# Four modulation blocks as matrix-vector products on TensorE, late squares on VectorE, and other slots for the later modulation blocks

## What is computed

```python
def ada_modulation(c, w, b, n_chunks):
    m = jax.nn.silu(c) @ w + b
    return jnp.split(m[:, None, :], n_chunks, axis=-1)
...
            shift, scale, gate = ada_modulation(c, a_ada_w[l], a_ada_b[l], 3)
            u = rms_norm(h, a_norm_g[l]) * (1 + scale) + shift
            q, k, v, z = jnp.split(u @ a_w_in[l], 4, axis=-1)
            q = rms_norm(q.reshape(bsz, seq, 2 * A_HEADS, A_HEAD_DIM), a_q_norm_g[l])
            k = rms_norm(k.reshape(bsz, seq, 2 * A_HEADS, A_HEAD_DIM), a_k_norm_g[l])
...
            o = diff_causal_attention(q, k, v, lam, slopes_a)
            o = rms_norm(o, a_subln_g[l]) * (1.0 - lambda_init)
            o = o.reshape(bsz, seq, A_INNER) * jax.nn.silu(z)
            h = h + gate * (o @ a_w_out[l])
            if layer == N_A_LAYERS - 1:
                kv_shift, kv_scale = ada_modulation(c, kv_ada_w, kv_ada_b, 2)
```

## Time and profile before

| | |
|---|---|
| runs | 1184.56 us median of 3 (1182.88 to 1186.97) |
| the profiled execution | 1183.36 us |
| its span | 1181.6 us |
| TensorE matmul | busy 1114.6 us (94%), 6120 |
| VectorE | busy 760.5 us (64%), 2483 |
| ScalarE | busy 666.3 us (56%), 2041 |
| GpSimd | busy 151.3 us (13%), 293 |
| chain that ended last | TensorE 85%, VectorE 6%, ScalarE 3%, issue 3%, DMA 2% |

### The profile page before, as it was taken

One profiled execution on the slowest core, in us unless ns is written; L12 is line 12 of the kernel. 1 busy time (PEld: TensorE's weight loads), 2 busy tenths in 40 slices (PEclk: granted clock), 3 DMA queues, 4 the chain that ended last, 5 costly groups with the idle time before them and its releaser, 6 DMA issues.

```text
span 1181.6 us, 19499 instructions
## 1 busy us (share of the span) xinstructions
PE 1114.6 (94%) x6120; PEld 887.1 (75%) x6120; DVE 760.5 (64%) x2483; ACT 666.3 (56%) x2041; POOL 151.3 (13%) x293
## 2 busy tenths in 40 slices
PE   1578999999999999999998999989999999999998
PEld 1466777777777777777777788878878778787887
DVE  6786787878878777877877444665555555556222
ACT  4565565666666566665665544666666666666010
POOL 1110111111111111011110111211111111110211
PEclk9988999999999999999999999999999999999999
DMA  9621222322223232222313634301111111113542
GB/s 360 226 81 50 87 73 87 97 64 81 80 90 95 72 100 66 88 81 88 98 54 95 199 102 131 125 19 35 45 43 41 41 41 41 41 50 112 161 143 89
DMA packets 65606, 108.47 MB, mean 92 GB/s; under 512 B 5600, under 2 KB 34400, under 8 KB 65248
## 3 DMA queue, kind: packets, MB, share of 16 engines
q1 hardware_dynamic: 65504, 107.23, 28.8%
HBM read 90.43 MB, written 16.78 MB: 91 GB/s over the span
## 4 chain that ended last, share of the span: by engine, by line
PE 85%; DVE 6%; ACT 3%; issue 3%; DMA 2%; SPq 1%; POOL 0%; DVEq 0%; ACTq 0%; POOLq 0%
PE ps_p L562 15%; PE ps_p L564 14%; PE ps_p L563 14%; PE ps_s L621 6%; PE ps_o L673 6%; PE ps_p L606 5%; PE ps_p L608 5%; PE ps_p L607 5%; PE ps_o L754 4%; PE ps_t L693 3%; PE ps_o L800 2%; PE ps_t L783 2%; PE ps_s L733 2%; DMA ada_in<-ada_w 1%; PE ps_o L647 1%
## 5 line engine op out<-in xcount | busy, mean ns | idle before, releaser
L562 PE MATMUL ps_p<-w_hi,u_hi 128*128 128x512 f32 x768 | 337.7, 440 | 21.9 <-DVE u_lo L1228 21.9
L564 PE MATMUL ps_p<-w_hi,u_lo 128*128 128x512 f32 x768 | 304.5, 396 | 0.0
L563 PE MATMUL ps_p<-w_lo,u_hi 128*128 128x512 f32 x768 | 303.9, 396 | 0.0
L562 PEld LDWEIGHTS ps_p<-w_hi,u_hi 128*128 128x128 f32 x768 | 146.5, 191 | 66.9 <-issue 23.2
L564 PEld LDWEIGHTS ps_p<-w_hi,u_lo 128*128 128x128 f32 x768 | 146.0, 190 | 32.9
L563 PEld LDWEIGHTS ps_p<-w_lo,u_hi 128*128 128x128 f32 x768 | 147.3, 192 | 17.4
L958 ACT ACTIVATE e<-e,negm 128x256 f32<-128x256 f32 (+7 forms) x128 | 98.4, 769 | 82.8 <-DVE negm L1293 81.6
L1182 DVE TENSOR_TENSOR w_lo<-raw,w_hi 128x512 fp32r<-128x512 f32 x120 | 82.8, 698 | 43.0 <-ACT w_hi L869 43.0
L495 POOL TENSOR_SCALAR gbuf<-gbuf 128x128 f32<-128x128 f32 (+1 forms) x96 | 32.9, 343 | 541.9 <-ACT gbuf L896 541.9
L995 ACT ACTIVATE pT<-ps_t 128x512 f32<-128x512 f32 (+2 forms) x96 | 44.5, 490 | 75.1 <-PE ps_t L693 74.6
L673 PE MATMUL ps_o<-va,pT 128*128 128x128 f32 x576 | 78.4, 281 | 0.0
(11 more groups left out here) (184 smaller groups left out, 2148.9 us busy)
## 6 DMA issues: line engine op xcount, KB each, us to landing
adabuf<-ada_w SPq DMA_DIRECT2D x48, 512.0 KB, 3.9
raw<-w_a SPq DMA_DIRECT2D x76, 256.0 KB, 3.9
raw<-w_b SPq DMA_DIRECT2D x44, 256.0 KB, 3.1
ada_in<-ada_w SPq DMA_DIRECT2D x7, 1024.0 KB, 13.4
x_in<-x SPq DMA_DIRECT2D x8, 512.0 KB, 12.5
oa_scratch<-gbuf SPq DMA_DIRECT2D x64, 64.0 KB, 1.6
late<-oa_scratch SPq DMA_DIRECT2D x8, 512.0 KB, 4.5
stage<-x SPq DMA_DIRECT2D x8, 512.0 KB, 4.9
```

The lines of the kernel that those rows point to most:

```text
L562: pe.matmul(o, u_hi[:, c, t], w_hi[par][:, c, :], start=(c == 0), stop=False)
L563: pe.matmul(o, u_hi[:, c, t], w_lo[par][:, c, :], start=False, stop=False)
L564: mm = pe.matmul(o, u_lo[:, c, t], w_hi[par][:, c, :], start=False, stop=(c == KD - 1))
```

## The change

Four of the first 16 blocks (1, 4, 7, 10) are computed on TensorE: their weights are stored transposed, TensorE multiplies each of a block's eight 128 x 128 parts with one column of silu(c), and VectorE adds the bias to the four columns at once. Weight chunks 0 to 3 and x tiles 2 and 3 are loaded behind the last block. The roots of x tiles 0 and 1 are made after block 5 instead of 3, those of tiles 2 and 3 behind the splits of the first head's weights instead of after block 8, with their squares and normalising on ScalarE. ScalarE and VectorE split all weight chunks behind smod; VectorE modulates x tile 1 before the low parts. The squares of x tiles 4 to 7 go to VectorE, two ahead of the attention and two in slot 1. The 48 later blocks are not worked on in the first head; the other heads have seven each, in slots 0 to 6, and the last has six.

```diff
-ADA_UNIT = 6
+ADA_UNIT = 7
+ADA_LATER = 48
+
+ADA_PE = (1, 4, 7, 10)
...
+def later_block(u, i):
+
+    k = ADA_UNIT * (u - 1) + i
+    return k if u > 0 and i < ADA_UNIT and k < ADA_LATER else None
...
-                    if is_a and live(0) and i < ADA_UNIT:
-                        k = ADA_UNIT * u + i
+                    if is_a and live(0) and later_block(u, i) is not None:
+                        k = later_block(u, i)
...
             for j in range(0, ADA0 - 2, 2):
                 sp.dma_start(ada0_in[:, j:j + 2, :], ada_w[j:j + 2].rearrange("a p n -> p a n")).then_inc(ada0_loaded[j // 2], 16)
-                if j < 8:
+                if j < 4:
                     load_x(j // 2)
-                if j in (8, 10):
-                    for c in (j - 8, j - 7):
-                        load_chunk(0, c, w_a[0, :, c, :])
             for j in (ADA0 - 2, ADA0 - 1):
                 sp.dma_start(ada0_in[:, j, :], ada_w[j]).then_inc(ada0_loaded[j + 1 - ADA0 // 2], 16)
+            for c in range(RAW):
+                load_chunk(0, c, w_a[0, :, c, :])
+            for n in (2, 3):
+                load_x(n)
             for c in range(RAW, KD):
                 load_chunk(0, c, w_a[0, :, c, :])
...
+            for j in ADA_PE:
+                pe.wait_ge(ada0_loaded[j // 2], 16)
+                for d in range(KD):
+                    mm = pe.matmul(ps_p[:, 0, j:j + 1], ada0_in[:, j, d * P:(d + 1) * P], csil[:, d:d + 1],
+                                   start=(d == 0), stop=(d == KD - 1))
+                mm.then_inc(s_ctr, 1)
             for n in range(2):
...
                     if isinstance(u, int) and u == 0 and 1 <= i < NT - 1:
                         x_modulate(i + 1)
+                        if i == 1:
+                            x_seed(2)
...
-            for k in range(2):
+            def x_rows_done(k):
                 for n in range(*x_groups[k]):
                     x_squares(n)
                 x_seed(k)
                 for n in range(*x_groups[k]):
                     x_normalise(k, n)
-            for c in range(RAW):
-                split_hi(0, c, 0)
+
+            x_rows_done(0)
             act.wait_ge(s_mod, 1)
             x_modulate(0)
-            for c in range(RAW, KD):
+            for c in range(2):
                 split_hi(0, c, 0)
             x_modulate(1)
-            for n in range(*x_groups[2]):
-                x_squares(n)
-            x_seed(2)
+            for c in range(2, KD):
+                split_hi(0, c, 0)
+            x_rows_done(1)
             attn_a(a, A_HEADS, 0)
...
+            def x_squares(n):
+
+                dve.wait_ge(n_x[n], 16)
+                dve.wait_ge(n_ss, n)
+                dve.tensor_tensor_reduce(e1[:, :].rearrange("p (a n) -> p a n", n=FW), x_rows(n), x_rows(n), 1.0, 0.0,
+                                         ALU.mult, ALU.add, xss[:, n:n + 1]).then_inc(n_ss, 1)
...
                     if first and 1 <= i < NT - 1:
                         x_modulate(i + 1)
+                    if first and i == 1:
+                        x_squares(6)
+                        x_squares(7)
+                        x_roots(2)
...
-                    if live(0) and i < ADA_UNIT:
-                        k = ADA_UNIT * u + i
+                    if live(0) and later_block(u, i) is not None:
+                        k = later_block(u, i)
...
             for j in range(ADA0):
-                dve.wait_ge(ada0_loaded[max(j // 2, j + 1 - ADA0 // 2)], 16)
-                modulation(ada0_in[:, j, :], j, ada0_done)
-                if j in (3, 8):
-                    x_roots((j - 3) // 5)
+                if j not in ADA_PE:
+                    dve.wait_ge(ada0_loaded[max(j // 2, j + 1 - ADA0 // 2)], 16)
+                    modulation(ada0_in[:, j, :], j, ada0_done)
+                if j == 5:
+                    x_roots(0)
...
-                if j >= ADA0 - RAW:
-                    split_lo(0, j - ADA0 + RAW, 0)
-            dve.wait_ge(ada0_done, ADA0)
+
+            dve.wait_ge(s_ctr, 1 + len(ADA_PE))
+            t = slice(ADA_PE[0], ADA_PE[-1] + 1, 3)
+            dve.tensor_tensor(mod[:, t], ps_p[:, 0, t], prm[:, C_ADAB + t.start:C_ADAB + t.stop:3], ALU.add).then_inc(ada0_done, 1)
+            dve.wait_ge(ada0_done, ADA0 - len(ADA_PE) + 1)
...
             x_modulate(0)
+            x_modulate(1)
             x_low(0)
-            for c in range(RAW, KD):
+            for c in range(KD):
                 split_lo(0, c, 0)
-            x_modulate(1)
             x_low(1)
-            x_roots(2)
+            x_roots(1)
+            dve.wait_ge(bias_step, 2)
+            x_squares(4)
+            x_squares(5)
             attn_a(a, A_HEADS, 0, M_A_GATE, 0)
```

More of the change, by code:

```diff
@@ L1621, in _ @@
             x_modulate(0)
+            x_modulate(1)
             x_low(0)
-            for c in range(RAW, KD):
+            for c in range(KD):
                 split_lo(0, c, 0)
-            x_modulate(1)
             x_low(1)
-            x_roots(2)
+            x_roots(1)
+            dve.wait_ge(bias_step, 2)
+            x_squares(4)
+            x_squares(5)
             attn_a(a, A_HEADS, 0, M_A_GATE, 0)
-            dve.wait_ge(ada_done, ADA_UNIT * A_HEADS)
+            dve.wait_ge(ada_done, ADA_LATER)
             dve.scalar_tensor_tensor(out=smod[:, 1, :], in0=mod[:, M_KV_SCALE:M_KV_SCALE + KD], scalar=1.0,
@@ L1661 @@
     ada_w = np.concatenate([f["a_ada_w"][0], f["kv_ada_w"], f["b_ada_w"][0]], axis=1)
-    ada_w = ada_w.T.reshape(-1, P, D)
+    ada_pe = ada_w.reshape(KD, P, -1, P).transpose(2, 1, 0, 3).reshape(-1, P, D)
+    ada_w = ada_w.T.reshape(-1, P, D).copy()
+    ada_w[list(ADA_PE)] = ada_pe[list(ADA_PE)]
     wa_in = f["a_w_in"][0].reshape(D, 4, A_HEADS, P).transpose(0, 2, 1, 3).reshape(D, 4 * D)
```

## The result

The changed kernel takes 1176.72 us, median of 8 runs (1174.74 to 1180.13); beside it on the same chip the kernel before took 1184.33, median of 8 (1178.61 to 1186.97). The ratio is 0.9948 [0.993, 0.9966]: **faster by 7.6 us**, clear of the noise though only 0.5%, where 2.9 were forecast. The median lies 1.9 us under the low end of the range. The profiled execution took 1174.74 us, the fastest of the eight. The changed kernel's times stand in groups (four at 1174.7 to 1175.3, two at 1178.1, then 1179.3 and 1180.1), so the median depends on how many runs fell into which. In a later session of 12 runs the median was 1179.44 against 1183.62 (experiment 9); over all 23 executions of this kernel it is 1178.40, against 1183.65 over 77 of the kernel before (one more of those, a slow one at 1269.59, is left out). The typical gain is thus about **5.2 us**.

A forecast was written before the change was run, and what follows sets the result against it. It took TensorE as the bound in seven heads, and waits in the opening and first head. 2.2 us to tile 1's end plus 0.7 from the clock made 2.9 off the median 1184.56: 1181.7 us, range 1178.6 to 1185.0.

The forecast's parts named there:

- the 7.8 us: Opening: modulation starts near 30.8 instead of 38.63; the queue behind smod leaves 1.6 us of it at x rows 2.
- an upper bound of 1.97: Opening: a modulation block on TensorE takes at most the 1.97 us of eight transposes; 1.9 us was taken, at no cost.
- the term 2.2: Up to the end of tile 1: query and key transposes at 58.3, 2.2 us earlier (1.7 to 2.8).
- I take the restart as slow until 50: Behind the hole in TensorE's queue: matmuls from 45.0 run at half clock until 50, between 48.7 and 51.1.
- the clock term 0.7: Slot 3: one idle stretch instead of two, so slow matmuls for nearer 3.8 than 5.8 us; 0.7 us gained.
- 1 us either way: Later slots of the first head: allowance on the total for where the clock falls there.
- Rival (1): Slot 3: the clock holds across the one idle stretch; gain 2.2 + 2.9 and 0.6, 1178.9 us; chance 0.15.
- Their going is worth nothing: Slots 3 to 5 of the first head: removing the later blocks gains nothing, as other chains set those slots.
- 0.6 us of idle time left: Heads 2 to 7: VectorE's 1.85 us idle covers the seventh block's 1.2 us, so it costs nothing.
- rival (4): Later heads: the seventh block delays the sums, qn and TensorE; 7.2 us lost, 2.9 gained, 1188.9 us; chance 0.05.
- (2): Restart behind the hole: TensorE runs at full pace from 45.0, tile 0 ends 2.4 us better; 1179.3 us; chance 0.08.
- (3): Opening: weights 4 to 7 come late, the hole is longer and eats the 2.9 us; 1184.5 us; chance 0.12.

The follow-up runs named there:

- experiment 9: The changed kernel again, unedited, in a later session: median 1179.44 us over 12 runs; its trace is of the fastest run.
- kernel 16: The kernel before, unedited, traced once more: 1183.30 us.
- kernel 6: The changed kernel with products of zeros in TensorE's idle stretches of the first head and 14 in the hole of slot 1: 1173.95 us.
- kernel 13: The changed kernel, unedited, another trace, from the middle group of times: 1177.83 us.
- kernel 1: The changed kernel with the later modulation blocks six a head again, from the first head on: 1181.20 us.
- 4: The kernel before with TensorE's idle stretches filled by 16, 16, 16 and 10 products that add zeros, which outlasted the stretches: 1182.88 us.
- kernel 2: The kernel before with only the later blocks moved, none in the first head and seven in the others: 1180.94 us.
- kernel 3: The kernel before with only the squares of x tiles 4 to 7 moved to VectorE, the roots behind them: 1185.16 us.
- 5: The kernel before with fewer products of zeros in TensorE's idle stretches (7, 8, 8 and 6): 1178.93 us.
- 12: The changed kernel with tile 0 projected whole before x rows 2 are transposed and the square of x tile 4 on ScalarE, without fillers: 1175.62 us.
- 14: The changed kernel, unedited, a further trace: 1179.33 us.
- 15: The changed kernel, unedited, a further trace: 1178.40 us.

## Why the prediction was wrong

The direction was right, and so was the working of the opening. Two terms of the sum were too small, and a loss was in no term. The median of the later session, 1179.44, lies inside the stated range; that would have been luck, for these errors partly cancel.

**Opening.** The last block was forecast to end at 30.3 and smod to be used at 30.8; it ended at 29.98 and the use came at 30.30. First matmul: 35.4, measured 34.95. Nine matmuls, then a hole until 45.0: a wait of 5.59 us until 44.43. qn: 54.4, measured 54.48 as its end. That most of the 7.8 us would go in the queue behind smod held: 8.3 us at smod, 2.2 at x rows 2. A block on TensorE took 3.5 us (6.99 for two, 3.57), where eight transposes gave an upper bound of 1.97. The bound was wrong: each of the eight products is recorded twice, so a block is 16 matmuls and 16 loads, not eight, and 16 loads at the pace of the row of eight make 3.9. It cost nothing, since block 10 ended at 26.1 and x rows 0 and 1 were transposed by 29.6, still before 30.30.

**To the end of tile 1**, the term 2.2. Measured: query and key transposes at 56.91 instead of 58.3, 3.6 us before the old 60.51. Of the 1.4 missed, 0.6 is the earlier restart; most of the rest is "I take the restart as slow until 50". The matmuls became fast at 48.27, 3.8 us after the restart, not 5.0. In the kernel before, 6.1 us had passed, in its slot 5, 3.8, and in kernel 16, the same program as before, 3.1 after the start at 42.38. So no one figure would have served; only the bounds could, and 3.8 lies near their early end. The hole was a loss that the change made for itself: the last of the nine matmuls ahead of it were fast, the first five behind it slow, and filling the hole (kernel 6) gave back 1.4 us at slot 3. The Trainium skill ("TensorE: Matmul & The Clock Gate", What's actually happening) says that half clock is the default and activity releases it; the trace agrees, with a clock of 0.50 at 42 and of 1.00 again from 50.

**From slot 3 on**, the clock term 0.7, is the step that failed. It said that the clock falls again at slot 3, for a shorter time, and dismissed the later slots with "1 us either way". In the profiled execution there was no fall at all from slot 3 to slot 8, worth 7.2 us. In typical ones there were two instead of four, worth 4.0, and there the step splits: at slot 3 it came true (slow matmuls for 4.1 us, 61.42 to 65.51 in kernel 13, and 0.94 gained where 0.7 was put), while the later slots gave 3.0. The same section did find that a single stretch of 2.36 us had cost 3.8 us of slow matmuls, and that was one of three places of falls behind slot 3 in the first head of the kernel before. None of the three was priced. Rival (1), that the clock holds, was priced for slot 3 alone and given 0.15; its time, 1178.9, is near the typical 1178.4, but by other terms: 3.95 and 3.98 gained, 2.5 given back. So that it came near is luck. The giving back was in no one's sum: the fall in layer 1 (at 1064 to 1074) stands in all five traces of the changed kernel and in neither of the two of the kernel before, behind the same 2.36 us. It is not the change's own, though: kernels 1 and 4 have it, and kernels 2, 3, 5 and 12 do not.

**The later blocks.** "Their going is worth nothing" held for the waits of slots 3 to 5: with the blocks there (kernel 1) the idle stretches of slots 5 and 6 are 2.31 and 2.29 us, without them 2.30 and 2.28. For slots 1 and 2 they were priced within the 2.2, and kernel 2 shows them worth 2.3 by themselves at slot 3. In time, their going is worth 2.7 us in the kernel before (kernel 2) and 2.8 in the changed one (kernel 1), half of the typical gain. It may act through the clock: of the traces without fillers, the falls of slots 6 and 7 stand in both of the kernel before and in kernel 1, which have the blocks, and in none of the nine without them; but kernel 3 has the blocks and, in its fastest run, not these falls. The waits do not tell why, and no experiment here separates it. The seventh block in the other heads costs nothing that can be seen, as forecast with 0.6 us of idle time left. From the scores of slot 8 to layer 1's wait it takes 955.1 to 955.3 us in the changed kernel, 954.4 and 954.5 before, but 955.3 in kernel 1 too, which has six a head. VectorE's row in the first of these heads:

```profile
170.78 0.42 DVE L1336 TENSOR_REDUCE ssum<-sq 128x4 f32<-128x256 f32 x1 [0.65 <-ACT sq L906]
```

So rival (4) did not come. Nor did (2): the restart was slow. Nor (3): the weights were on time.

**What stays open.** Why a stretch of 2.3 to 2.6 us loses the clock in one execution and not in another, with the same work around it. The traces of the changed kernel give one hint. In the two without a fall (the first, and kernel 9) the last of the nine matmuls ahead of the hole were already fast, from 38.2 on, and behind it they became fast at 48.3 to 48.6. In kernels 13, 14 and 15 none of the nine was fast, and behind the hole they became so at 47.8, 49.3 and 48.3 (14 and 15 being late by their transfer). And in 13 the matmuls of slot 3 were fast at first and slow only from 61.42 on, 1.7 us after TensorE had restarted at 59.67. In the kernel before, they were slow from the restart at 63.57. That looks as if the clock changed at moments that are not tied to the kernel's own steps, so that the same work meets them at another point. The Trainium skill ("TensorE: Matmul & The Clock Gate", What's actually happening) says that the chip's watch on TensorE's activity is free-running and does not reset when a kernel starts; the traces fit that, but none of them shows it, and no experiment here could shift it against the kernel. Nor is it explained why the stretch in layer 1 lost the clock in each trace of the changed kernel.

## What to carry to other kernels

Where TensorE's idle stretches are 1.6 to 2.6 us and the clock falls behind them, count every one: each was worth 1.3 to 2.6 us here, and a few products that add zeros in the stretch (8 in 2.3 us, not 16) took the fall away. Work moved off one engine only pays down to the next queue: of 8.3 us gained at smod, 2.2 arrived at the next transposes. Work that no wait ends on can still cost time: the blocks in the first head did, by a way that stayed open. When the times of a kernel stand in groups, take more runs before believing a median, and compare the milestones of traces from more than one group.

## What the runs showed of the hardware that was not expected

- A float32 product of 128 x 128 that is no transpose is recorded as two matmuls and took 0.23 us at full clock (3.73 us for 16), where a transpose of the same shape is one and takes 0.10 (0.80 us from the first of eight at 52.60 to the matmul behind them). A product of one column is recorded twice as well, and a block of eight took 3.57 us, in which the 16 loads were busy for 3.48: for one column the loads are the cost. The transposes right behind it took 1.95 us for eight, so this is at the lower pace; no run shows it at the full one.
- The clock's record and the matmuls can disagree. In kernels 13 and 15, the same program, the nine matmuls ahead of the hole were 0.43 us apart; the record reads 1.00 in the one (from 32 to 60) and 0.50 in the other (36 to 48).
- Equal idle stretches lose the clock in one execution and not in another, and the fall comes up to 1.7 us after the work has resumed. Two such falls (3.1 us) and, by one trace, a late transfer (1.5) make three groups of times out of one program.
